# A fused transformer kernel: the output projection of three pooled groups by seven block products a quad

## The reference, cut to what matters

```python
def pool_mixer(h, w_in, w_group, scale, w_out):
    u, z = jnp.split(h @ w_in, 2, axis=-1)
    p = causal_multiscale_pool(u).reshape(B, S, N_POOL_GROUPS, GROUP_WIDTH)
    y = jnp.einsum('bsgc,gcd->bsgd', p, w_group).reshape(B, S, A_WIDTH_2) * scale
    return (y * jax.nn.silu(z)) @ w_out
# in second_block:  x = x + gate[:, None, :] * y
```

## Time and profile before

| | us |
|---|---|
| median of 3 runs (2353.84 to 2354.54) | 2354.03 |
| the profiled execution | 2353.32 |
| its span | 2351.4 |
| TensorE busy / VectorE / POOL / ScalarE | 2324.9 / 1537.1 / 1255.9 / 859.8 |
| output stage of g = 1, 2, 3 | 43.5 each |

### The profile page before, as it was taken

How to read it: one execution, slowest core, us unless ns; L and a number is a source line. 1 busy time by engine, 2 the same in 40 slices (tenths; PEclk the granted TensorE clock), 3 DMA queues, 4 the chain that set the end, 5 groups by cost and what they waited for, 6 DMA issues and landing times.

```text
span 2351.4 us, 32286 instructions
## 1 busy us (share of the span) xinstructions
PE 2324.9 (99%) x11585; PEld 1943.6 (83%) x11585; DVE 1537.1 (65%) x1839; ACT 859.8 (37%) x1596; POOL 1255.9 (53%) x724
## 2 busy tenths in 40 slices
PE   9999999999999999999999999999999999999998
PEld 7888789888888888888888888788878788889887
DVE  7825555524578777877877777774672967147885
ACT  5212555512543222222222443122231244157773
POOL 4533954143135666676777424573754733467743
PEclk9999999999999999999999999999999999999999
DMA  6511001031011333333332211112121123210034
GB/s 220 157 45 50 19 19 37 1 117 54 10 42 50 117 125 125 117 124 125 117 123 63 63 45 45 59 57 73 54 81 62 58 67 110 79 37 25 22 112 139
DMA packets 67420, 179.08 MB, mean 76 GB/s; under 512 B 7010, under 2 KB 13924, under 8 KB 65200
## 3 DMA queue, kind: packets, MB, share of 16 engines
q1 hardware_dynamic: 57840, 148.03, 19.3%
q10 hardware_dynamic: 9104, 27.51, 3.5%
q0 software_dynamic: 368, 2.10, 0.5%
HBM read 161.84 MB, written 15.77 MB: 76 GB/s over the span
## 4 chain that ended last, share of the span: by engine, by line
PE 76%; DVE 6%; issue 4%; POOL 2%; ACT 1%; DMA 0%; POOLq 0%; DVEq 0%; ACTq 0%; SPq 0%
PE ps L705 21%; PE ps L706 21%; PE ps L708 21%; PE ps L855 4%; PE ps L833 3%; PE ps L843 2%; DVE trail L3538 1%; PE ps L2410 1%; POOL split_lo L1658 1%; PE ps L2426 1%; ACT p L956 1%; PE ps L2395 1%; PE ps L2396 1%; PE ps L2425 1%; PE ps L509 0%
## 5 line engine op out<-in xcount | busy, mean ns | idle before, releaser
L705 PE MATMUL ps<-h_hi,split_hi 128*128 128x512 f32 x1546 | 607.2, 393 | 3.4 <-DVE h_lo L3220 1.3
L706 PE MATMUL ps<-h_lo,split_hi 128*128 128x512 f32 x1546 | 601.9, 389 | 0.0
L708 PE MATMUL ps<-h_hi,split_lo 128*128 128x512 f32 x1546 | 536.5, 389 | 0.0
L1516 POOL TENSOR_TENSOR split_hi<-raw,cf 128x1024 fp32r<-128x1024 f32 x64 | 125.2, 1956 | 427.8 <-PE ps L708 373.2
L705 PEld LDWEIGHTS ps<-h_hi,split_hi 128*128 128x128 f32 x1546 | 290.9, 188 | 63.9 <-issue 2.2
L708 PEld LDWEIGHTS ps<-h_hi,split_lo 128*128 128x128 f32 x1546 | 290.9, 188 | 61.0
L706 PEld LDWEIGHTS ps<-h_lo,split_hi 128*128 128x128 f32 x1546 | 291.2, 188 | 56.3 <-issue 0.2
L1605 POOL TENSOR_TENSOR split_lo<-raw,split_hi 128x512 fp32r<-128x512 f32 x144 | 232.9, 1635 | 193.9 <-ACT split_hi L2723 193.4
L1658 POOL TENSOR_TENSOR split_lo<-raw,split_hi 128x512 fp32r<-128x512 f32 x84 | 128.1, 1534 | 179.2 <-ACT split_hi L2884 179.2
L2723 ACT CAST split_hi<-raw 128x512 fp32r<-128x512 f32 x144 | 86.7, 622 | 283.9 <-PE ps L708 204.0
L1518 POOL TENSOR_TENSOR split_lo<-raw,split_hi 128x1024 fp32r<-128x1024 f32 x64 | 178.4, 2787 | 5.0
(11 more groups left out here) (508 smaller groups left out, 5213.2 us busy)
## 6 DMA issues: line engine op xcount, KB each, us to landing
raw<-in_strips SPq DMA_DIRECT2D x208, 256.0 KB, 2.8
raw<-in_strips SPq DMA_DIRECT2D x86, 512.0 KB, 3.4
ada_raw<-in_ada SPq DMA_DIRECT2D x64, 512.0 KB, 3.7
memw_raw<-in_mem_strips SPq DMA_DIRECT2D x8, 512.0 KB, 6.1
xT<-in_xT ACTq DMA_DIRECT2D x4, 1024.0 KB, 8.1
x_spill_d<-xT ACTq DMA_DIRECT2D x1, 3584.0 KB, 10.1
xT<-x_spill_d ACTq DMA_DIRECT2D x2, 1792.0 KB, 9.9
out_T<-out_sb SPq DMA_DIRECT2D x13, 256.0 KB, 2.2
```

Of the source, the lines that this page charges most:

```text
L705: pe.matmul(acc[:, a:b], w_hi, hi[:, a:b], start=first, stop=False)
L706: pe.matmul(acc[:, a:b], w_hi, lo[:, a:b], start=False, stop=False)
L708: mm = pe.matmul(acc[:, a:b], w_lo, hi[:, a:b], start=False, stop=last)
L1516: pool.tensor_tensor(hi, raw[:, r, :], ones[:, 0:1].to_broadcast([P, D]), ALU.mult).then_inc(hi_split, 1)
```

## The change

The output projection of g = 1, 2, 3 is made in two quads of four output tiles (`out_quad`). In a quad, channel tiles 0, 1 against 2, 3, output tiles in two halves, and early (t1) against late (t2) tokens are blocked two by two, and seven block products are made instead of eight. A product has two parts (two output tiles), each 6 matmuls of 512 tokens in one bank of PSUM; products 2, 4, 5 and 6 add to a bank that holds an earlier product, after VectorE has added its state so far to x (`out_sum`, 14 a quad, 512 tokens each).

- Tokens: VectorE makes differences of gated halves in place (`first_difference`) and three combinations (`neg_two`, `neg_three`, `neg_four`, two tiles each); all with high and low parts. These lie for g = 1, 2 in the late half of the tiles 0 to 5 of h_hi and h_lo, for g = 3 in `pool_sums`.
- What is overwritten of h is stored once in g = 1 by six DMAs of 0.5 MB on ScalarE's queue, and fetched back for g = 2 and g = 3 by six each (`h_fetch`), then rounded in place on ScalarE (`h_round`, six roundings of 1024 columns). The fetches stand behind form 45 and behind form 3 of the next group, the roundings ahead of form 4 and behind forms 4 and 5.
- Weights: a quad has seven forms (32 to 38 and 39 to 45); POOL adds four blocks and makes seven low parts a quad instead of four low parts (`out_forms`). The last four forms alternate between places 2 and 3. The strips are laid out anew on the host; as many bytes are loaded.
- Key norm: tiles in the order 0, 2, 1, 3, 4, 6, 5, 7, squares in eight places of their own, additions mostly behind the output sums; the first key strip is rounded by ScalarE instead of POOL, its product takes seven tiles ahead of the norm's sum.
- TensorE's and POOL's loops over the groups are unrolled.

The core of the diff ("..." where lines are left out):

```diff
+GROUP_SLOT = [p % 4 for p in range(42)] + [2, 3, 2, 3]
+GROUP_BEFORE = [p - GROUP_FORMS for p in (40, 41, 44, 45)] + [max(q for q in range(p) if GROUP_SLOT[q] == GROUP_SLOT[p]) for p in range(4, 46)]
+OUT_BANKS = (((4, 6), (5, 7), (0, 1)), ((0, 2), (1, 3), (4, 5)))
+OUT_BANK = [0, 1, 0, 2, 0, 1, 0]
+OUT_AFTER = {2: 0, 4: 2, 5: 1, 6: 4}
+OUT_SECOND, OUT_LATE = (1, 4, 6), (1, 2, 4, 5)
+KV_ORDER = [0, 2, 1, 3, 4, 6, 5, 7]
...
+kv_squares = [sums_f32[:, t, :] for t in (1, 0, 2, 3, 10, 11)] + [last_tmp[:, t, :] for t in range(2)]
+n_kv = norm_plan(lambda k: xT[:, KV_ORDER[k], :], NK, None, kv_squares[0], rms5[:, :], stat_pair(1), columns=bank(0, QT), places=kv_squares)
...
+def load_out(g, quad):
+    for i, d in ((2, 0), (3, 1), (4, 2), (6, 3)):
+        group_split(sp, g, out_form(quad, i))
+        load_group_half(g, 12 + 2 * quad + d // 2, d % 2)
...
+def out_forms(g, quad):
+    j, at = 10 + 2 * quad, out_form(quad, 0)
+    group_half(pool, g, j, 0)
+    group_low(g, at, OUT_SOURCE[0])
+    group_half(pool, g, j + 1, 0)
+    group_half(pool, g, j + 1, 1)
+    pool.tensor_tensor(pool_form, a21, a22, ALU.add).then_inc(form_sum, 1)
+    group_low(g, at + 1, OUT_SOURCE[1])
+    summed(g, 4 + quad, 1)
+    pool.tensor_tensor(a21, a21, a11, ALU.subtract).then_inc(form_sum, 1)
+    group_split(pool, g, at + 1)
+    pool.tensor_tensor(pool_form, a11, pool_form, ALU.subtract).then_inc(form_sum, 1)
+    group_low(g, at + 2, OUT_SOURCE[2])
+    group_half(pool, g, j, 1)
+    group_split(pool, g, at + 2)
+    pool.tensor_tensor(pool_form, a12, pool_form, ALU.add).then_inc(form_sum, 1)
+    for i in range(3, 7):
+        group_low(g, at + i, OUT_SOURCE[i])
...
+def out_quad(g, quad):
+    for i in range(7):
+        p = out_form(quad, i)
+        group_split(pe, g, p)
+        if quad == 0:
+            if i in (2, 4, 6):
+                neg_lower(pe, g, i)
+            else:
+                gate_lower(pe, g, {0: 1, 1: 3, 3: 5, 5: 6}[i])
+        for part in range(2):
+            if i == 0 and quad == 0:
+                gate_made(pe, g, 1 + part)
+            elif i == 3 and quad == 0 and part == 0:
+                gate_made(pe, g, 3)
+            elif i == 0 and part == 0:
+                out_read(pe, g, 2 * 3 + 1)
+            elif i == 0:
+                gate_made(pe, g, 5)
+            elif i == 1 and quad == 1:
+                out_read(pe, g, 2 * 3 + 2)
+            elif i == 3 and quad == 1:
+                out_read(pe, g, 2 * 6 + 1)
+            elif i in OUT_AFTER:
+                out_read(pe, g, 14 * quad + 2 * OUT_AFTER[i] + part + 1)
+            slot, w = group_at(p)
+            product(pe, bank(OUT_BANKS[quad][OUT_BANK[i]][part]), slot,
+                    [(w + 2 * part + kk, *out_token(g, i, kk)) for kk in range(2)], HALF, start=i in (0, 1, 3), skip=True)\
+                .then_inc(form_done if part else pool_tile, 1)
...
+        elif n == 5 and g > 1:
+            pe.wait_ge(h_rounded, 6 * (g - 2) + 2)
+            if g > 1:
+                pe.wait_ge(h_rounded, 6 * (g - 1))
...
+out_read(pe, POOL_GROUPS - 1, 22)
+product(pe, pair(2), S_KV % 2, h_pieces(KV_ORDER[:7]), before=as_split(pe, sp_kv), stop=False)
+out_read(pe, POOL_GROUPS - 1, 28)
+product(pe, pair(2), S_KV % 2, h_pieces(KV_ORDER[7:]), before=lambda j: split_there(pe, sp_kv, KV_ORDER[7 + j]), start=False)
...
+def h_fetch(m, done):
+    a = NEG_T[m]
+    for low in range(2):
+        act.dma_start(h_plain[:, NK * low + a:NK * low + a + 2, HALF:T], h_keep_d[:, low, a:a + 2, :]).then_inc(done, 16)
+def h_round(m):
+    for low, of in enumerate((h_hi, h_lo)):
+        a = NEG_T[m]
+        act.copy(of[:, a:a + 2, HALF:T], h_plain[:, NK * low + a:NK * low + a + 2, HALF:T]).then_inc(h_rounded, 1)
...
+    if g > 1:
+        act.wait_ge(h_again, 64 + 64 * (g - 1))
+        h_round(2)
-            gated_high_tile(g, 2)
-            gated_high_tile(g, 3)
+            out_high(g, 3, 2, slice(0, T))
+            neg_high_tile(g, 2, 1, 4)
+            neg_high_tile(g, 3, 1, 5)
+        if p == GROUP_OUT_AT + 4:
+            out_high(g, 4, 3, out_tokens[1])
+            out_high(g, 5, 3, out_tokens[0])
+            neg_high_tile(g, 4, 1, 6)
...
-        if p in (32, 33):
-            gated_high_tile(g, p - 32)
-        if g == POOL_GROUPS - 1 and p >= 36:
-            key_square(p - 36)
+        if p == GROUP_OUT_AT:
+            out_high(g, 1, 0, slice(0, T))
+        if p == GROUP_OUT_AT + 1:
+            out_high(g, 2, 1, slice(0, T))
+            if g == 1:
+                act.wait_ge(h_kept, 64 + 96)
+            act.copy(neg_whole(g, 3, slice(0, 2)), gates[:, 0:2, out_tokens[0]]).then_inc(pool_yhi, 1)
+        if p == GROUP_OUT_AT + 2:
+            for m in range(3):
+                neg_high_tile(g, 2 + m, 0, 1 + m)
+        if g == 1 and p in (8, 10, 12, 14, 16, 18):
+            m, low = 2 + (p - 8) // 4, (p - 8) // 2 % 2
+            sums_made(act, 1, 12)
+            act.dma_start(h_keep_d[:, low, NEG_T[m]:NEG_T[m] + 2, :],
+                          rows((h_hi, h_lo)[low][:, NEG_T[m]:NEG_T[m] + 2, HALF:T])).then_inc(h_kept, 16)
+        if g > 1 and p == 4:
+            h_round(3)
+        if g > 1 and p == 5:
+            act.wait_ge(h_kept, 64 + 96 + 32 * (g - 1))
+            h_round(4)
+        if p == GROUP_FORMS - 1 and g < POOL_GROUPS - 1:
+            h_fetch(2, h_again)
+            h_fetch(3, h_again)
+        if p == GROUP_FORMS + 3:
+            h_fetch(4, h_kept)
+        if g == POOL_GROUPS - 1 and p == GROUP_FORMS - 1:
+            act.wait_ge(raw_loaded[0], 16 * (S_KV // 2 + 1))
+            act.copy(split_hi[:, 0, :, :].rearrange("p a n -> p (a n)"), raw[:, 0, :]).then_inc(hi_split, 1)
+        if g == POOL_GROUPS - 1 and out_form(1, 2) <= p < out_form(1, 6):
+            key_square(p - out_form(1, 2))
...
+def first_difference(g, t):
+    link(gate_step(g, t))
+    dve.tensor_tensor(gated_tile(t)[:, t2], gated_tile(t)[:, t2], gated_tile(t)[:, t1], ALU.subtract).then_inc(pool_g, 1)
...
+def neg_two(g, kk):
+    dve.tensor_tensor(neg_full(g, 2, kk), gated_tile(kk)[:, t2], gated_tile(2 + kk)[:, t2], ALU.subtract).then_inc(neg_sum, 1)
+def neg_three(g, kk):
+    gate_high(dve, g, 3)
+    neg_made(dve, g, 1 + 3 * kk)
+    dve.tensor_tensor(neg_full(g, 3, kk), neg_full(g, 2, kk), neg_full(g, 3, kk), ALU.add).then_inc(neg_sum, 1)
+def neg_four(g, kk):
+    dve.tensor_tensor(neg_full(g, 4, kk), neg_full(g, 2, kk), gated_tile(2 + kk)[:, t1], ALU.add).then_inc(neg_sum, 1)
+def neg_low(g, m, kk):
+    neg_high(dve, g, m - 1 + 3 * kk)
+    neg_made(dve, g, m - 1 + 3 * kk)
+    dve.tensor_tensor(neg_tile(g, m, 1, kk), neg_full(g, m, kk), rows(neg_tile(g, m, 0, kk)), ALU.subtract).then_inc(neg_lo, 1)
...
+    if i in (3, 4, 5):
+        out_read(dve, g, 14 * quad + 2 * {3: 0, 4: 1, 5: 2}[i] + part + 1)
+    o, tok = 4 * quad + 2 * part + (i in OUT_SECOND), out_tokens[i in OUT_LATE]
+    dve.scalar_tensor_tensor(out=xT[:, o, tok], in0=bank(OUT_BANKS[quad][OUT_BANK[i]][part]), scalar=adav[:, 16 + o:17 + o],
+                             in1=xT[:, o, tok], op0=ALU.mult, op1=ALU.add).then_inc(pool_res, 1)
...
+def out_tokens_made(g):
+    first_difference(g, 0)
+    first_difference(g, 1)
+    gates_low(g, 3, y_lo[:, 0:2, t1], gates[:, 0:2, t1], y_hi[:, 0:2, t1])
+    gate_step(g, 2).then_inc(pool_g, 1)
+    if g == 1:
+        dve.wait_ge(h_kept, 64 + 96)
+    gate_made(dve, g, 3)
+    neg_two(g, 0)
+    neg_three(g, 0)
+    difference_low(g, 0)
+    neg_four(g, 0)
+    neg_low(g, 2, 0)
+    gate_step(g, 3, t2).then_inc(pool_g, 1)
+    gate_made(dve, g, 4)
+    neg_two(g, 1)
+    neg_three(g, 1)
+    difference_low(g, 1)
+    gate_step(g, 3, t1).then_inc(pool_g, 1)
+    gate_made(dve, g, 5)
+    neg_four(g, 1)
+    neg_low(g, 2, 1)
+    out_sum(g, 0, 0, 0)
+    out_sum(g, 0, 0, 1)
+    gates_low(g, 4, y_lo[:, 2, :], gated_tile(2), gated_hi_tile(2))
+    gates_low(g, 6, y_lo[:, 3, t1], gated_tile(3)[:, t1], gated_hi_tile(3)[:, t1])
+    out_sum(g, 0, 1, 0)
+    out_sum(g, 0, 1, 1)
+    neg_low(g, 3, 0)
+    neg_low(g, 3, 1)
+    out_sum(g, 0, 2, 0)
+    out_sum(g, 0, 2, 1)
+    gates_low(g, 5, y_lo[:, 3, t2], gated_tile(3)[:, t2], gated_hi_tile(3)[:, t2])
+    out_sum(g, 0, 3, 0)
+    out_sum(g, 0, 3, 1)
+    neg_low(g, 4, 0)
+    neg_low(g, 4, 1)
+    out_sum(g, 0, 4, 0)
+    out_sum(g, 0, 4, 1)
...
+    out_tokens_made(g)
+    for quad in range(2):
+        for i in range(7) if quad else (5, 6):
+            for part in range(2):
+                out_sum(g, quad, i, part)
+                if g == POOL_GROUPS - 1 and quad and i == 5 and part == 1:
+                    key_low(4)
+            if g == POOL_GROUPS - 1 and quad and i < 4:
+                key_low(i)
+            if g == POOL_GROUPS - 1 and quad and i == 4:
+                norm_add(dve, n_kv, 1)
+            if g == POOL_GROUPS - 1 and quad and i == 5:
+                norm_add(dve, n_kv, 2)
+key_low(5)
+for k in range(3, 7):
+    norm_add(dve, n_kv, k)
+key_low(6)
```

(2 more changed lines are left out.)

186 lines of the change are left out of this document (116 added, 70 removed).

## The result

The changed kernel takes **2371.61 us** (median of 4 runs, 2369.37 to 2374.02), the kernel before 2354.28 (4 runs, 2353.84 to 2354.98): ratio **1.0074, 95% interval 1.0056 to 1.0091**, some 17 us. That is outside the predicted range. The profiled run took 2371.14 us with a span of 2369.3.

The account below looks back on a forecast made before the run. TensorE was taken to bound the kernel. Matmuls saved -16.3, quad 0 gaps +10.8, transitions +1.0 and tail +5.0 summed to +0.5 us: profile 2353.8, median 2354.5, range 2343 to 2361; no difference had 39%.

Parts of the forecast that it names:

- Bound and removed work: Whole kernel: TensorE bounds it; 24 matmuls fewer a group at 0.2267 us save 5.44, 16.3 us in three.
- Quad 0: First quad of each output stage: TensorE waits before products 1 to 4, 3.6 us a group, 10.8 in three.
- 0.7 + 0.7 + 0.7 + 0.6: VectorE before product 1: gate 3 of late tokens, neg two, neg three, lower half; given as 3.85, 1.15 us lost.
- The exclusion between VectorE's two-input work and POOL's: Two-input SBUF work on VectorE and POOL's work exclude each other; sums out of PSUM go through.
- From group to group: Two transitions between groups, with fetches and roundings of stored tokens: 0.5 us each, 1.0 in all.
- Four land by T+4, in time: ScalarE's four 0.5 MB fetches, issued at T-4.6, land by T+4; T is TensorE's start of the next group.
- 0.5 each: Loss at each of two transitions, with form 4 ready at 11.2 where needed at 10.9; 1.0 us in all.
- an upper bound of 2.5 us: Transition's upper bound, if the strips' 2.8 us landing doubles beside the fetches.
- Rival B: Stored tokens come late, ScalarE waits for fetches, TensorE behind it: 3 to 3.5 us a transition, 2360.5 us; 28%.
- The tail: After group four's last product: VectorE's norm additions and lower halves delay the first key strip, 5.0 us (3.2 to 7.2).
- Half of these meet: Tail: half of VectorE's operations there meet POOL's longer ones on the key strips, hence 5.0 us.
- Rival A: Output stages' gaps stay small, POOL's work falling beside VectorE's sums out of PSUM: 2342 to 2345 us; 33%.

Follow-up runs that it names:

- e3_quiet: Changed kernel with POOL's seven lower halves of quad 0 covering 8 of 512 columns, groups two to four; 2365.62 us, ratio 1.0053 to the kernel before.
- e2_round_only: Changed kernel without the fetches of stored tokens and their waits, ScalarE's roundings kept; 2363.31 us, ratio 1.0043 to the kernel before.
- e8_filler: Changed kernel with 29 unread matmuls added in TensorE's gaps at the end; 2369.18 us, ratio 1.0073 to the kernel before.
- e6_between: Changed kernel with earlier squares and norm additions, the second key strip's first four pieces put between the first's; 2368.96 us, ratio 1.0071.
- c2_bin: Changed kernel with SyncE issuing the fetches, key strips interleaved, the next two strips reordered and an earlier high part; 2356.92 us, ratio 1.0019.

## Why the prediction was wrong, step by step

**Bound and removed work: right.** TensorE's time was the span's, and 72 matmuls went (11585 to 11513). What was missed: in group four's output stage a matmul whose operands come from `pool_sums` follows after 0.233 us, not 0.2267 (twelve from 1932.43 to 1935.23); with 72 such matmuls that is about half a microsecond. Those from `h_hi` in group two's stage keep 0.2267 (twelve from 1640.43 to 1643.15).

**Quad 0: the mechanism right, its size nearly.** Predicted 1.15, 1.1, 0.8 and 0.6 us in front of products 1 to 4; the trace has 0.85, 0.75, 1.02 and 0.23, which with 0.25 each is 3.85 us lost against 3.6. (The prediction's own terms in front of product 1, 0.7 + 0.7 + 0.7 + 0.6, are 2.7 and not 3.85; counted from +1.1 they end at 3.8, so its 1.15 is 1.1.) The exclusion between VectorE's two-input work and POOL's, from which the walk was made, is what e3_quiet took away: 2.85 to 0.34. The profile puts the third gap down to POOL's lower half:

```profile
1616.18 1.29 POOL L1721 TENSOR_TENSOR split_lo<-raw,split_hi 128x512 fp32r<-128x512 f32 x1 [5.79 <-ACT split_hi L3002]
...
1623.44 0.47 PE L764 MATMUL ps<-p_hi,split_hi 128*128 128x512 f32 x1 [1.02 <-POOL split_lo L1721]
```

But product 3 uses form 35, whose low part is the one at 1616.18, done at 1617.47. What ended just before the matmul is the pair of `y_lo` at 1619.87, drawn out to 3.48 us beside POOL's lower halves for products 4 and 5 and done at 1623.35. So it is VectorE's lower halves, as predicted, and the same in groups three and four.

**From group to group: the step that failed.** "Four land by T+4, in time" and "0.5 each" took the landing times of lone transfers for four that leave together, and asked only whether the fetched tokens come in time. They did. What came late was the strip half beside them, at 5.9 us. It was in the text, but as an upper bound of 2.5 us, priced as one late form; the trace shows that POOL, once its lead is gone, loses at most of the later quads against the trailing means, and that the longest gaps cost clock. Out of the periods: 4.13 + 5.44 - 3.85 = 5.7 us for the first transition and 7.91 + 5.44 - 3.85 = 9.5 for the second (3.4 of it clock), 15.2 against the predicted 1.0. By the experiments 12.5 of these are the fetches', 1.8 the roundings', and 0.9 stay without a return. Rival B had the consequence (the strips slowed) but through a wait of ScalarE for the fetch, and with less than half of the size on average (3 to 3.5 a transition against 7.6).

**The tail: the mechanism right, the size at the bound.** Predicted 5.0 us, bounds 3.2 to 7.2; the gaps are 7.0, and with 0.75 behind them and 1.7 of clock 9.5. "Half of these meet" was wrong: the first addition, the lower half at 1957.78 (2.70 for 1.28) and, at 1938.84, a lower half before (2.16) all met POOL. That a gap has a clock behind it stood in no term and no bound. Of the 20.5 us, the transitions are 14.2 more than forecast, the end 4.5 and the stages' first quads 0.8; with the forecast's own 0.5 that is 20.0.

**Rival A** failed as the forecast said it would: the stages' gaps are not small.

Open: how deep the clock falls behind the same gap. It lost 1.7, 5.1 and 12 us in three profiles with nearly the same gap of 3.9 to 4.7 us at the end, and no run told what decides it. It is not a property of the kernel alone: the four executions of e2_round_only took 2359.8, 2363.2, 2363.4 and 2368.5 us at mean granted clocks of 0.997, 0.996, 0.996 and 0.993. Open too is how the fetches' 12.5 us divide between the slowed strip loads and the hold on ScalarE.

## What to carry to other kernels

A transfer that "lands in time" can still be the cost: ask which small load, with a consumer waiting, is issued beside it, and put the bulk behind that load in the same engine's order; here this took 12.5 us of the periods down to 1.9. Where a saving on the bounding engine is paid with two-input SBUF work on VectorE and POOL at once, count them as one engine. Look at what ended just before a gap closed, not only at the engine that a row names. By the rows of this kernel, price an idle gap of TensorE at its length and 0.25 us more, and one near 2 us or longer at up to some us of clock besides.

## What the runs showed of the hardware that was not expected

- Three transfers of 256 KB landed after 5.9 us (median) beside 0.5 MB fetches from another engine's queue, 2.6 us when the fetches stood behind them in SyncE's own order.
- Issuing four transfers held ScalarE for 2.47 us; four fetches on SyncE took 3.61 us from 1652.01 on and held up nothing, since its next strip load was due only at 1662.64.
- A gap costs more than its figure, as the rows overlap and the second start behind it is late too: 1.10 us lost for 0.85.
- VectorE and POOL hold each other up by whole operations: 1.28 us on VectorE became 3.38 and 3.50 beside POOL's of 2.47 and 2.39.
- The granted clock fell behind a gap of 1.84 us in one profile (0.70 from 1665 to 1670, e8_filler), and stayed at 1.00 behind gaps of 2.03 (e6_between) and 3.04 us (c2_bin) in others; with the gap at the end filled by matmuls that nobody reads it stayed at 1.00.
